# The last block's hidden activations: from TensorE transposes to VectorE block transposes and a DRAM bounce

## The reference

```python
D_FF = 5632
def swiglu(h, w_in, w_out):
    g, u = jnp.split(h @ w_in, 2, axis=-1)
    return (jax.nn.silu(g) * u) @ w_out
...
    x = x + mix
    x = x + swiglu(rms_norm(x, ffn_norm[layer]), w_ffn_in[layer], w_ffn_out[layer])
return rms_norm(x, final_norm)
```

## Time and profile before

| | us |
|---|---|
| median of 3 runs (lowest, highest) | 2028.17 (2028.09, 2028.22) |
| the profiled execution's own time | 2028.79 |
| its span, first to last instruction | 2027.0 |
| TensorE busy in it | 2007.7 |
| VectorE busy | 1647.8 |
| ScalarE busy | 1178.9 |
| granted TensorE clock, mean | 0.998 of full |

### The profile page before, as it was taken

One profiled execution on the slowest core, in us unless ns is written; L12 is line 12 of the kernel. 1 busy time (PEld: TensorE's weight loads), 2 busy tenths in 40 slices (PEclk: granted clock), 3 DMA queues, 4 the chain that ended last, 5 costly groups with the idle time before them and its releaser, 6 DMA issues.

```text
span 2027.0 us, 24678 instructions
## 1 busy us (share of the span) xinstructions
PE 2007.7 (99%) x9278; PEld 1666.3 (82%) x9278; DVE 1647.8 (81%) x1556; ACT 1178.9 (58%) x1195; POOL 170.5 (8%) x216
## 2 busy tenths in 40 slices
PE   8999999999999999999999999999999999999998
PEld 6888888888888888888888887788888888888886
DVE  5656767779999999999986467779999999999995
ACT  6744655555665555656556466555656556655554
POOL 0000000100111101111100000100111101111010
PEclk9999999999999999999999999999999999999999
DMA  7755443866998888988888644676988889988885
GB/s 262 226 176 167 158 153 127 278 202 224 269 268 248 242 247 260 267 253 253 243 245 229 188 148 146 213 224 231 267 252 255 243 249 267 263 256 240 247 261 159
DMA packets 237187, 461.40 MB, mean 228 GB/s; under 512 B 16480, under 2 KB 21376, under 8 KB 236992
## 3 DMA queue, kind: packets, MB, share of 16 engines
q1 hardware_dynamic: 202832, 386.97, 56.7%
q0 software_dynamic: 30496, 69.22, 16.9%
q10 hardware_dynamic: 3792, 4.34, 0.7%
HBM read 401.10 MB, written 17.29 MB: 206 GB/s over the span
## 4 chain that ended last, share of the span: by engine, by line
PE 90%; DVE 5%; ACT 2%; DMA 1%; issue 1%; ACTq 0%; SPq 0%; DVEq 0%
PE ps L1715 58%; PE ps L1499 28%; DVE g_lo L1248 1%; PE ps L1606 1%; DVE w_lo L902 1%; DMA raw<-in_w_ab_in 1%; DVE w_lo L1253 1%; DVE w_sum L1236 0%; PE ps L1866 0%; ACT w_hi L464 0%; PE ps L1525 0%; PE ps L1841 0%; ACT junk L507 0%; ACT probs L830 0%; DVE w_sum L1234 0%
## 5 line engine op out<-in xcount | busy, mean ns | idle before, releaser
L1248 DVE TENSOR_TENSOR g_lo<-g_raw,g_hi 128x2048 fp32r<-128x2048 f32 x240 | 547.4, 2288 | 54.0 <-ACT g_hi L715 31.0
L902 DVE TENSOR_TENSOR w_lo<-raw,w_hi 128x1024 fp32r<-128x1024 f32 x248 | 294.7, 1221 | 155.0 <-ACT w_hi L464 153.6
L715 ACT CAST g_hi<-g_raw 128x2048 fp32r<-128x2048 f32 x140 | 265.6, 1912 | 156.2 <-PE ps L1715 150.3
L464 ACT ACTIVATE w_hi<-raw 128x1024 fp32r<-128x1024 f32 x248 | 253.6, 1056 | 143.2 <-DMA raw<-in_w_ab_in 53.3
L708 ACT CAST g_hi<-g_raw 128x2048 fp32r<-128x2048 f32 x100 | 191.5, 1915 | 218.6 <-DVE g_raw L1230 218.6
L1715 PE MATMUL ps<-g_hi,xT_hi 128*128 128x512 f32 x780 | 303.6, 389 | 0.6 <-DVE w_lo L1253 0.6
L1715 PE MATMUL ps<-g_hi,xT_lo 128*128 128x512 f32 x780 | 303.4, 389 | 0.0
L1499 PE MATMUL ps<-w_hi,xT_hi 128*128 128x512 f32 x672 | 265.3, 395 | 1.8 <-DVE xT_lo L921 1.1
L1715 PE MATMUL ps<-g_lo,xT_hi 128*128 128x512 f32 x680 | 264.5, 389 | 0.0
L1499 PE MATMUL ps<-w_hi,xT_lo 128*128 128x512 f32 x672 | 262.3, 390 | 0.0
L1499 PE MATMUL ps<-w_lo,xT_hi 128*128 128x512 f32 x672 | 262.1, 390 | 0.0
(11 more groups left out here) (222 smaller groups left out, 3041.2 us busy)
## 6 DMA issues: line engine op xcount, KB each, us to landing
g_raw<-in_w_ffn_in SPq DMA_DIRECT2D x320, 512.0 KB, 4.8
g_raw<-in_w_ffn_out SPq DMA_DIRECT2D x160, 512.0 KB, 4.7
raw<-in_w_ab_in SPq DMA_DIRECT2D x96, 512.0 KB, 4.8
x<-y POOLq DMA_DIRECT2D x80, 512.0 KB, 6.7
raw<-in_w_qkv SPq DMA_DIRECT2D x40, 512.0 KB, 4.5
raw<-in_w_ab_out SPq DMA_DIRECT2D x32, 512.0 KB, 4.8
raw<-in_w_ffn_in SPq DMA_DIRECT2D x32, 512.0 KB, 4.6
raw<-in_w_c_out SPq DMA_DIRECT2D x32, 512.0 KB, 4.7
```

The costliest lines, as they stand in the source:

```text
L464: act.activation(w_hi[:, s, :], raw[:, s % RAWS, :], ACT.Copy).then_inc(hi_ready, 1)
L715: act.copy(dst[:, 0:4, :].rearrange("p s w -> p (s w)"), src[:, :, :].rearrange("p s w -> p (s w)")).then_inc(group_hi_ready, 1)
L902: dve.tensor_tensor(w_lo[:, s, :], raw[:, s % RAWS, :], w_hi[:, s, :], ALU.subtract).then_inc(lo_ready, 1)
L1248: ins = dve.tensor_tensor(lo_part[:, 0:4, :].rearrange("p s w -> p (s w)"), src[:, :, :].rearrange("p s w -> p (s w)"), hi_part[:, 0:4, :] ...
```

## The change

The hid of block 10 goes the way of the others. `turn_hidden`, `hT_his` and `hT_los` are gone. In the last body, ScalarE makes silu before group 11's hi part, and VectorE makes hidden and turns it before group 11's lo part. POOL's order in the last body becomes carry_out, add_y 0, carry_in, add_y 1, add_y 2, add_y 3. ScalarE's rows_hi stands after the hi parts of chunks 3 to 5 of the W2 round, and VectorE's rows_lo after their lo parts. h1T_hi moves to another place in SBUF, since hid_rows now occupies its own. Semaphore targets count FB turns per layer instead of FB - 1 (those lines are left out below).

```diff
-              (sb("h1T_hi", [P, 4, T], F32R, at=bias_at + 72 * KB), sb("h1T_lo", [P, 4, T], F32R, at=bias_at + 22 * KB))]
+              (sb("h1T_hi", [P, 4, T], F32R, at=bias_at + 50 * KB), sb("h1T_lo", [P, 4, T], F32R, at=bias_at + 22 * KB))]
...
@@ POOL
                 for f in range(1, FB):
-                    add_y(f - 1, layer, 0)
                     if f < FB - 1:
+                        add_y(f - 1, layer, 0)
                         carry_out(f, layer)
-                    add_y(f - 1, layer, 1)
-                    if f < FB - 1:
+                        add_y(f - 1, layer, 1)
                         carry_in(f, layer)
+                    else:
+                        carry_out(f, layer)
+                        add_y(f - 1, layer, 0)
+                        carry_in(f, layer)
+                        add_y(f - 1, layer, 1)
                     add_y(f - 1, layer, 2)
                     add_y(f - 1, layer, 3)
...
@@ ScalarE
-            def hT_his(f, layer, hT_hi):
-
-                for b in range(2):
-                    act.wait_ge(ht_done, 2 * layer + b + 1)
-                    for h in range(2):
-                        ins = act.copy(hT_hi[:, 2 * b + h, :], PAIR[2][:, b, h * T:(h + 1) * T])
-                    ins.then_inc(hh_ready, 1)
...
                     hi_(10)
+                    if last:
+                        silu(f, layer, base)
                     hi_(11)
-                    silu(f, layer, base)
...
+                    if not last:
+                        silu(f, layer, base)
...
                 his(last, 0, 3)
                 copy_y(FB - 2, layer, 2)
-                hT_his(FB - 1, layer, hT[1][0])
                 act.wait_ge(group_used, group_at(layer, FB - 1) + 11)
                 his(last, 3, 6)
+                rows_hi(FB - 1, layer, hT[1][0])
                 copy_y(FB - 2, layer, 3)
...
@@ VectorE
                     out_parts(f, layer)
-                    group(f, layer, 11)
+                    if not last:
+                        group(f, layer, 11)
                     hidden(f, layer, base)
-                    if not last:
-                        turn_blocks(f, layer)
+                    turn_blocks(f, layer)
+                    if last:
+                        group(f, layer, 11)
...
                 dve.wait_ge(group_used, used + 1)
-                los(last, 2, 3)
-                hT_los(FB - 1, layer, *hT[1])
-                los(last, 3, 4)
+                los(last, 2, 4)
                 dve.wait_ge(group_used, used + 2)
                 los(last, 4, 6)
+                rows_lo(FB - 1, layer, *hT[1])
...
@@ TensorE
-            def turn_hidden(f, layer):
-
-                pe.wait_ge(hid_ready, f * 2 + (2 * FB * layer + 2))
-                for b in range(2):
-                    for h in range(2):
-                        for t in range(NT):
-                            c = (2 * b + h) * P
-                            ins = pe.transpose(PAIR[2][:, b, h * T + t * P:h * T + (t + 1) * P], hid[:, t, c:c + P], ident)
-                    ins.then_inc(ht_done, 1)
...
-                        if last and g == BLOCK_GROUPS - 1:
-                            turn_hidden(f, layer)
```

More of the change, by code:

```diff
@@ L262, in trunk @@
         silu_ready, hid_ready = sem("silu_ready"), sem("hid_ready")
-        ht_done, hh_ready, hT_ready = sem("ht_done"), sem("hh_ready"), sem("hT_ready")
+        hh_ready, hT_ready = sem("hh_ready"), sem("hT_ready")
         hid_turned, hid_out, hid_in = sem("hid_turned"), sem("hid_out"), sem("hid_in")
@@ L404, in carry_out @@
             def carry_out(f, layer):
-                pool.wait_ge(hid_turned, f + (layer * (FB - 1) + 1))
+                pool.wait_ge(hid_turned, f + (layer * FB + 1))
                 pool.dma_start(hid_dram, hid_blk[:, :, :, :, :].rearrange("p j k t b -> p j (k t b)")).then_inc(hid_out, 16)
             def carry_in(f, layer):
-                pool.wait_ge(hid_out, f * 16 + (layer * (FB - 1) + 1) * 16)
+                pool.wait_ge(hid_out, f * 16 + (layer * FB + 1) * 16)
                 if f:
@@ L680, in rows_hi @@
             def rows_hi(f, layer, hT_hi):
-                act.wait_ge(hid_in, f * 64 + (layer * (FB - 1) + 1) * 64)
+                act.wait_ge(hid_in, f * 64 + (layer * FB + 1) * 64)
                 act.copy(hT_hi[:, :, :].rearrange("p k (t i b) -> p (k t) i b", t=NT, i=4),
                          hid_rows[:, :, :, :, :].rearrange("p i k t b -> p (k t) i b")).then_inc(hh_ready, 2)
-            def hT_his(f, layer, hT_hi):
-                for b in range(2):
-                    act.wait_ge(ht_done, 2 * layer + b + 1)
-                    for h in range(2):
-                        ins = act.copy(hT_hi[:, 2 * b + h, :], PAIR[2][:, b, h * T:(h + 1) * T])
-                    ins.then_inc(hh_ready, 1)
             def free_group(f, layer, g, first, base):
@@ L720, in copy_p1 @@
                 act.wait_ge(group_used, f * BLOCK_GROUPS + (group_at(layer, 0) + LAST_STRASSEN + 1))
-                act.wait_ge(hid_turned, f + layer * (FB - 1))
+                act.wait_ge(hid_turned, f + layer * FB)
                 act.copy(gu[:, 0, :], ps[:, 0, :]).then_inc(p1_copied, 1)
@@ L744, in ffn, with block @@
                 ahead(base + 1, 7)
-                def block(f, first):
+                def block(f, first, last):
                     def hi_(g):
@@ L772, in block @@
                     hi_(10)
+                    if last:
+                        silu(f, layer, base)
                     hi_(11)
-                    silu(f, layer, base)
-                block(1, True)
-                block(2, False)
+                    if not last:
+                        silu(f, layer, base)
+                block(1, True, False)
+                block(2, False, False)
                 with act.Fori(3, FB - 1) as f:
-                    block(f, False)
-                block(FB - 1, False)
+                    block(f, False, False)
+                block(FB - 1, False, True)
                 copy_y(FB - 2, layer, 0)
@@ L1174, in turn_blocks @@
                 if not isinstance(f, int) or f + layer > 0:
-                    dve.wait_ge(hid_out, f * 16 + layer * (FB - 1) * 16)
+                    dve.wait_ge(hid_out, f * 16 + layer * FB * 16)
                 for t in range(NT):
@@ L1186, in rows_lo @@
                                   ALU.subtract).then_inc(hT_ready, 2)
-            def hT_los(f, layer, hT_hi, hT_lo):
-                for b in range(2):
-                    dve.wait_ge(hh_ready, f * 2 + (2 * FB * layer + b + 1))
-                    for h in range(2):
-                        ins = dve.tensor_tensor(hT_lo[:, 2 * b + h, :], PAIR[2][:, b, h * T:(h + 1) * T],
-                                                hT_hi[:, 2 * b + h, :], ALU.subtract)
-                    ins.then_inc(hT_ready, 1)
             def sum_tokens(layer):
@@ L1762, in ffn, with block @@
                 chunks(base + 1, 0, 8, *X, PAIR[1])
-                def block(f, first, last):
+                def block(f, first):
                     for g in range(BLOCK_GROUPS):
@@ L1789, in block @@
                             plain_group(g, g == 0, g == N_UP - 1)
-                block(1, True, False)
+                block(1, True)
                 with pe.Fori(2, FB - 1) as f:
-                    block(f, False, False)
-                block(FB - 1, False, True)
+                    block(f, False)
+                block(FB - 1, False)
             ffn(0, R_F0, {1: turning(1, 3, ABO_PAIRS)})
```

## The result

The changed kernel took 2036.97 us (median of 6 runs, 2035.55 to 2040.02); the kernel before took 2028.2 us (6 runs, 2027.66 to 2029.03). The ratio is 1.0043, with a 95% interval of 1.0033 to 1.0053: slower by 8.8 us, where 2.8 were forecast, and above the forecast range of 2027.0 to 2034.3 us. The profiled execution took 2037.47 us with a span of 2035.7, 8.7 us above that of before.

The account below looks back on a forecast made before the run. TensorE, busy 99% of the span and 90% of the chain, was taken to bound the kernel. Transposes -1.8 and stall +4.6 gave net +2.8 on 2028.17, so 2031.0 us; range 2027.0 to 2034.3.

Parts of the forecast that it names:

- The price of the transposes: At the end of group 11, removing TensorE's eight transposes saves 0.89 us in layer 0 and 0.92 in layer 1.
- The cover of group 11: VectorE's lo part ready by about 1064.3, TensorE wants it at 1072.56: no cost, 8 us of cover.
- The cover of the bounce: Hid_blk's trip out and back by DMA: all ins down by 1074.5 to 1076, before ScalarE asks for them.
- POOL's late adds: Adds of y after the reordering: add 1 lands near 1084 instead of 1078; cover of a few us, priced at nothing.
- (b): Ahead of the W2 round, chunk 5's landing, then hi, lo, rows_lo: shift +1.37 and +1.40 us; last if t over 4.2.
- t: Latency of chunk 5's load from issue to landing, taken as 4.8 us; bounds 3.8 and 7.0 (layer 0), 5.9 (layer 1).
- t - 3.43: Layer 0's shift of the W2 round's start in us, given t; forecast +1.37.
- t - 3.40: Layer 1's shift of the W2 round's start in us, given t; forecast +1.40.
- Chain (a): Ahead of the W2 round, VectorE's three lo parts and rows_lo in a row: stall 1.65 us, shift +0.76 and +0.73.
- Rival 2: At the W2 round, no stall or one made up later; only the transposes felt: -1.8 us, 2026.4; chance 0.07.
- Rival 1: Chunk 5's load stays slow, the bounce's DMA traffic replacing add 1: +6.1 us, 2034.3; chance 0.28.
- (c): After the W2 stall, TensorE's later work moves by the same amount; POOL's late adds are priced at nothing.

Follow-up runs that it names:

- rows first: The changed kernel with rows_hi and rows_lo moved ahead of the hi and lo parts of chunks 3 to 5 in both layers: 2026.49 us, 0.9990 of the kernel before.
- the run with the bounce unused: The changed kernel with hid still sent out and read back by DMA, but h1T made by TensorE's transposes as before: 2028.54 us, 1.0000 of the kernel before.

## Why the prediction was wrong

**Right.** The price of the transposes: rows first is 1.7 to 2.2 us under the kernel before, against 1.8. The cover of group 11: its lo part was done at 1063.3, and TensorE wanted it near 1072. The cover of the bounce: all reads had landed by 1071.45, and ScalarE reached rows_hi at 1077.83. POOL's late adds hold up nothing, as the run with the bounce unused shows. The place of the wait and its releaser were right, and so was it that (b), the landing of chunk 5, ends last. With t = 5.5 in layer 0 the formula t - 3.43 gives +2.07, measured +1.98; with t = 8.3 in layer 1 t - 3.40 gives +4.90, measured +4.73. Chain (a) alone, less one lo part, comes to a wait of some 0.45 us by the prediction's numbers and measured 0.21. Rival 2 is refuted. Rival 1 is what happened in its outcome, a chunk 5 that lands late, but not in its cause, which was to be the bounce's traffic; and its bounds of 7.0 and 5.9 us, 2034.3 in time, were too low.

**Wrong, first step: t of chunk 5.** "Add 1 no longer runs at that time" was the sentence that failed. I had let add 0 take 6.4 us and the fourth read 4.4 to 6, the latter from executions with three reads beside it, and put add 1 at 1076. Add 0 took 5.4 us in layer 0, the read, alone, took 2.9, add 1 began at 1071.79 and 1990.31, and t was 5.5 and 8.3, not 4.8. The bound I took for layer 1, 5.9, came from an execution in which the add had begun 3.0 us ahead of the load; a load issued within half a us of the add had no row in my sum. This is 0.6 + 3.3 = 3.9 us of shift. With the add held back, t was 4.9 and 4.5, so the quiet figure itself was sound. The Trainium skill (DMA: Bandwidth & Descriptors, "Queues, rings and completion order") has each DMA engine take its queue rows in turn. The 8.1 to 8.3 us beside the add, against 4.5 and 4.9 without it, agree with that; the 5.1 to 5.9 us that half of the loads took beside the same add are not explained by it. I had noted that the rule favoured rival 1 and then not followed it.

**Wrong, second step: the stall was priced at its length.** In (c) each us of stall cost one us. The lower clock behind it cost 2.4 us in layer 1. Filled with work, the same wait gave 2.0 us back. A gap made on purpose cost 2.75 us beyond its length by the medians, and 1.5 by the matmuls of its trace. The 8.7 us of the spans are thus 2.8 as forecast, 3.9 from t and 2.4 from the clock, less the 0.5 of head start: 8.6. The Trainium skill (TensorE: Matmul & The Clock Gate, "HAM oscillation — how this bites in real kernels") says that waits of TensorE return it to its lower clock, which the work after pays for. The waits of 5.48 and 6.50 us agree, and one of 2.12; those of 2.70 and 3.09 had no slow matmul behind them.

**Open.** No run shows what makes chunk 5 take 5 or 8 us beside the add. The traces of the changed kernel and of six experiments have a full add 1 issued within half a us of chunk 5's load, in two layers each. In seven of these 14 cases the load took 5.1 to 5.9 us, in the other seven 7.7 to 8.5. Issued 0.3 to 0.4 us ahead of the add, it took 5.5 to 5.9 in all four cases. With the add ahead no such order holds: in layer 1 the add was always some 0.4 us ahead, and the load took 5.1, 5.8 and five times 8.2 to 8.5. In the kernel before, chunk 4 of layer 0 was issued 0.7 us behind an add and landed after 4.2 us, a case that the prediction did not read. Nor is it shown when a short idle lowers the clock.

## What to carry to other kernels

When a result moves to a longer way, put the instructions that deliver it at the earliest place in each in-order stream at which their inputs are surely there, ahead of any prefetch work whose own input is a load; here one place was worth 9.4 us, and the earliest place 10.5. When a DMA queue is reordered, write down what the first freed transfer will start beside, with the shortest latencies seen and not the usual ones: by the trace's order of events, which was not tried by itself, it was add 0 and then a read, both landing early (5.4 and 2.9 us), that put the add beside the load. And a stall on TensorE can cost more than its length, 0 to 2.75 us more here, so a forecast that has one should carry a term for the clock after it.

## What the hardware showed beyond that

- Two DMAs of 512 KB from different queues, chunk 5's load and add 1, issued within half a us of each other: the add took 8.4 to 10.1 us in 14 cases, against 4.8 us for the add at 1980.65 of the kernel before, with no load issued in that time. The load took 5.1 to 5.9 us in seven of them and 7.7 to 8.5 in seven, against 4.9 and 4.5 with the add held back. More loads of the same queue were in flight in all of these cases.
- The length of an idle did not by itself decide on the clock: 2.12 us lowered it, 2.70 and 3.09 us didn't; after 5.48 us twelve matmuls were slow, after 6.50 us some seven.
